# A Strassen stream of split weights: two blocks per x pair, weight sums on the DMA queue, and M2 added onto ScalarE's copy of M1

## The reference

```python
    proj = h @ w_in[l]
...
    x = x + mixed @ w_o[l]
    hx = rmsnorm(x, norm_x_g[l])
    hm = rmsnorm(mem, norm_mem_g[l])
    xq = (hx @ w_xq[l]).reshape(b, s, XATTN_HEADS, XATTN_HEAD_DIM)
...
    x = x + (jax.nn.silu(hf @ w_gate[l]) * (hf @ w_up[l])) @ w_down[l]
```

## Time and profile before

| | us |
|---|---|
| median of 3 runs | 2067.45 (2067.3 to 2068.65) |
| span of the profiled execution, first to last instruction | 2065.9 |
| TensorE matmuls busy | 2054.4, 99% of the span, 9334 instructions |
| VectorE busy | 1667.2 (81%) |
| ScalarE busy | 1181.2 (57%) |
| POOL busy | 50.0 (2%) |

### The profile page before, as it was taken

The page is one execution under the profiler, slowest core; times in us unless marked ns, Lnnn a source line. Parts: engine busy times, 40 slices in busy tenths (PEclk is TensorE's granted clock), DMA queues, the critical chain, the costliest instruction groups (busy, mean ns, idle before and its releaser), DMA issues.

```text
span 2065.9 us, 25348 instructions
## 1 busy us (share of the span) xinstructions
PE 2054.4 (99%) x9334; PEld 1699.8 (82%) x9334; DVE 1667.2 (81%) x1830; ACT 1181.2 (57%) x1533; POOL 50.0 (2%) x84
## 2 busy tenths in 40 slices
PE   9999999999999999999999999999999999999998
PEld 8888888888888888888888888888788888888787
DVE  6877778867766788989889898898777778988875
ACT  7666557656655565555555555555756655654453
POOL 1000000000000000000000000000000000000000
PEclk9999999999999999999999999999999999999999
DMA  9555557655544458777777777776465567789763
GB/s 347 180 172 184 184 180 259 225 182 184 189 158 153 159 185 300 267 259 242 243 237 259 261 242 243 236 270 213 158 214 178 180 201 234 269 285 329 219 197 109
DMA packets 219259, 453.74 MB, mean 220 GB/s; under 512 B 14449, under 2 KB 17153, under 8 KB 219009
## 3 DMA queue, kind: packets, MB, share of 16 engines
q1 hardware_dynamic: 213232, 432.07, 62.9%
q0 software_dynamic: 5616, 19.94, 3.0%
q10 hardware_dynamic: 288, 0.13, 0.0%
HBM read 447.88 MB, written 4.19 MB: 219 GB/s over the span
## 4 chain that ended last, share of the span: by engine, by line
PE 95%; DVE 2%; ACT 1%; issue 1%; DMA 1%; POOL 0%; SPq 0%; DVEq 0%; POOLq 0%; ACTq 0%
PE ps L1117 30%; PE ps L1119 30%; PE ps L1118 29%; PE ps L687 2%; DVE wlo L2494 1%; PE ps L837 1%; PE ps L817 1%; PE ps L921 0%; DMA FR<-in_post_norm_g_dram 0%; PE ps L952 0%; PE ps L963 0%; PE ps L901 0%; DMA FR<-in_x_t_dram 0%; ACT whi L1718 0%; DVE raw L2507 0%
## 5 line engine op out<-in xcount | busy, mean ns | idle before, releaser
L2494 DVE TENSOR_TENSOR wlo<-raw,whi 128x1024 fp32r<-128x1024 f32 x835 | 1010.4, 1222 | 262.8 <-ACT whi L1718 257.4
L1718 ACT ACTIVATE whi<-raw 128x1024 fp32r<-128x1024 f32 x835 | 876.6, 1058 | 564.5 <-PE ps L1119 518.2
L1117 PE MATMUL ps<-whi,bh 128*128 128x512 f32 x1384 | 547.3, 395 | 2.3 <-DVE wlo L2494 2.1
L1119 PE MATMUL ps<-whi,bl 128*128 128x512 f32 x1384 | 539.9, 390 | 0.0
L1118 PE MATMUL ps<-wlo,bh 128*128 128x512 f32 x1384 | 539.2, 390 | 0.0
L1117 PE MATMUL ps<-whi,ah 128*128 128x512 f32 x1080 | 429.3, 398 | 0.2 <-DVE wlo L2494 0.2
L1119 PE MATMUL ps<-whi,al 128*128 128x512 f32 x1080 | 421.6, 390 | 0.0
L1118 PE MATMUL ps<-wlo,ah 128*128 128x512 f32 x1080 | 420.9, 390 | 0.0
L1117 PEld LDWEIGHTS ps<-whi,bh 128*128 128x128 f32 x1384 | 260.1, 188 | 57.0 <-DVE wlo L2494 3.1
L1119 PEld LDWEIGHTS ps<-whi,bl 128*128 128x128 f32 x1384 | 259.8, 188 | 54.7
L1118 PEld LDWEIGHTS ps<-wlo,bh 128*128 128x128 f32 x1384 | 260.2, 188 | 52.5 <-issue 0.2
(11 more groups left out here) (264 smaller groups left out, 1334.6 us busy)
## 6 DMA issues: line engine op xcount, KB each, us to landing
raw<-in_w_in_dram SPq DMA_DIRECT2D x168, 512.0 KB, 4.5
raw<-in_w_ada_dram SPq DMA_DIRECT2D x96, 512.0 KB, 4.6
raw<-in_w_gate_dram SPq DMA_DIRECT2D x88, 512.0 KB, 4.9
raw<-in_w_up_dram SPq DMA_DIRECT2D x88, 512.0 KB, 5.4
raw<-in_w_down_dram SPq DMA_DIRECT2D x88, 512.0 KB, 5.4
raw<-in_w_merge_dram SPq DMA_DIRECT2D x64, 512.0 KB, 5.0
raw<-in_w_o_dram SPq DMA_DIRECT2D x32, 512.0 KB, 4.8
raw<-in_w_xk_dram SPq DMA_DIRECT2D x32, 512.0 KB, 4.7
```

The lines of the kernel that those rows point to most:

```text
L1117: e.matmul(o, xh[:, k, tokens], wh, start=first, stop=False, skip_group_check=more)
L1119: ins = e.matmul(o, xl[:, k, tokens], wh, start=False, skip_group_check=more, stop=kk == 1 and (st.end or st.form in READ))
L1718: done(e.activation(split_at(n)[0], place(item), ACT.Copy), "hi")
L2494: done(e.tensor_tensor(lo, place(stream.entries[n].item), hi.bitcast(F32), ALU.subtract), "lo")
```

## The change

Five things change together.

1. For the pairs of x (kinds tq, v and rg: five pairs) `_pair` lays out **two** Strassen blocks, over chunks 0 and 1, with two of each product, and two chunks instead of three as normal entries. A second set of forms, `x1`, is made for chunk 1 of x. TensorE has 30 matmuls fewer (8610 rows in its program before, 8580 now).
2. Weight sums of the kinds in `QUEUED` are DMAs with an add, issued by POOL (`add_weights`): M5's and M4's, and M6's too in the x pairs. Of 180 sums (160 before) 60 go this way; 120 stay on VectorE. The adding DMA reads both items and writes one of them.
3. In the x pairs four spare item buffers lie in X, which is loaded twice: for its squares, and again after the last spare item is taken.
4. ScalarE copies M1 straight into the bank of the second panel's tile 0, and M2 adds onto it (`start` is left out). The second panel has no `side` any more; it is read straight from PSUM.
5. In pairs of three or two chunks a normal entry stands ahead of M6 and M2.

```diff
+QUADS = {"tq": 2, "v": 2, "rg": 2}
+QUEUED = ("tq", "v", "rg", "o", "xk", "xv", "xq", "xo", "q", "ga", "pu", "gp", "out")
+SPARES = 4
+LANDING = 3
...
+        quads = min(QUADS.get(self.panels[f].kind, 1), chunks - 1)
+        places = [[self._item(p, c, hf) for p, hf in ((f, 1), (f, 0), (s, 0), (s, 1))] for c in range(quads)]
+        todo = iter([(c, hf) for c in range(quads, chunks) for hf in range(2)])
+        at = [{} for _ in range(quads)]
...
+        def product(form, k, start=False, **more):
+            b22, b12, b11, b21 = places[k]
+            item, add = {"M5": (b12, b11), "M3": (b22, None), "M1": (b11, None), "M6": (b22, b12), "M2": (b21, None),
+                         "M7": (b11, b22), "M4": (b21, b22)}[form]
+            at[k][form] = n = self._entry(item, add)
             panel, tile, _, half, _ = PRODUCTS[form]
-            self._step(n, (f, s)[panel], 0, half, (tile,), form, **more)
...
+        if quads == 1:
+            product("M5", 0, start=True, job=False)
+            product("M3", 0, start=True, job=False)
+            normal(f, *next(todo), snap=("s5", q))
+            product("M1", 0, start=True, job=False)
+            if chunks == 4:
+                normal(f, *next(todo), snap=("s1", q))
...
+            product("M5", 0, start=True, job=False)
+            product("M5", 1, job=False)
+            product("M3", 0, start=True)
+            normal(f, *next(todo), snap=("s5", q))
+            product("M3", 1, job=False)
+            product("M1", 0, start=True, job=False)
+            product("M1", 1)
             normal(f, *next(todo), snap=("s1", q))
-            product("M6", b22, b12)
-            product("M2", b21, start=True, snap=("v", q))
-            normal(f, *next(todo))
-            normal(f, *next(todo))
-        else:
-            product("M2", b21, start=True, snap=("s1", q))
-            product("M6", b22, b12)
+            product("M2", 0, job=False)
+            product("M6", 0)
...
+            product("M2", 1, job=False)
+            product("M7", 0)
+            product("M7", 1)
+            normal(f, *next(todo), snap=("s3", q))
+            product("M4", 0, aside=q)
...
+            if quads == 2 and i == 0:
+                product("M4", 1)
...
+        queued = self.panels[f].kind in QUEUED
+        early = 2
+        if self.panels[f - 1].stagger == "first":
+            early = 3 if queued else 1
+        elif queued:
+            early = 1 if q == 0 else 6
+        for k, made in enumerate(at):
+            for form, n in (("M5", made["M5"] - early), ("M6", made["M3"] + 1),
+                            ("M7", made["M1"] + 2 if quads == 1 else made["M6"] + 1),
+                            ("M4", max(made["M2"], made["M6"]) + 1)):
+                self.sums[made[form]] = Sum(n, made, k, form, queued and form in (("M5", "M4") if quads == 1 else ("M5", "M6", "M4")))
...
+        for m, one in self.sums.items():
+            for item in (self.entries[m].item, self.entries[m].add):
+                used(item, (one.before, 1))
+                used(item, (one.before + (LANDING if one.queue else 0), 1))
...
-            at = min(range(RAWS), key=lambda r: (-1, 0) if holds[r] is None else last[holds[r]])
+            fit = [r for r in range(number) if r < RAWS or (self.spares[r - RAWS].first <= first[item][0]
+                                                            and last[item][0] < self.spares[r - RAWS].last)]
+            at = min(fit, key=lambda r: (-1, r < RAWS) if holds[r] is None else last[holds[r]])
...
+        def ready_to_sum(e, m):
+
+            made, form = stream.sums[m].pair, stream.sums[m].form
+            if form == "M5":
+                for item in stream.entries[m]:
+                    e.wait_ge(*loaded(item))
+            else:
+                e.wait_ge(*sum_done(made["M5" if form == "M6" else "M6"]))
+                e.wait_ge(s["lo"], made[{"M6": "M3", "M7": "M1", "M4": "M2"}[form]] + 1)
...
-            which = 2 * role[p][0] + t
-            return None if which == 3 else side[:, which, :]
...
-                if st.form in ("M6", "M4"):
-                    e.wait_ge(s["snap"], 3 * q + (2 if st.form == "M6" else 3))
+                if st.form in ("M2", "M6", "M4"):
+                    e.wait_ge(s["snap"], 3 * q + (3 if st.form == "M4" else 2))
...
-                form, place = {"s5": ("M5", (0, 0)), "s1": ("M1", (1, 0)), "s3": ("M7", (0, 1))}[what]
-                pair, at = stream.pairs[q]
+                form = {"s5": "M5", "s1": "M1", "s3": "M7"}[what]
+                (f, second), at = stream.pairs[q]
                 panel, t = PRODUCTS[form][:2]
                 e.wait_ge(s["half"], at[form] + 1)
-                if q:
-                    e.wait_ge(*side_taken(stream.pairs[q - 1][0][place[0]], place[1]))
-                done(e.activation(side_of(pair[place[0]], place[1]), bank_of(pair[panel], t)[:, :], ACT.Copy), "snap")
+                if what == "s1":
+                    dst = bank_of(second, 0)[:, :]
+                    if stream.nth[second] > 1:
+                        e.wait_ge(*ev_before(second, 0))
+                else:
+                    tile = 1 if what == "s3" else 0
+                    dst = side_of(f, tile)
+                    if q:
+                        e.wait_ge(*side_taken(stream.pairs[q - 1][0][0], tile))
+                done(e.activation(dst, bank_of((f, second)[panel], t)[:, :], ACT.Copy), "snap")
 
...
+                for k in range(4):
+                    ins = e.activation(AF["x1"][:, k, :], XT[1][:, k, :], ACT.Copy, scale=gcols("mix", 1)[k])
                 done(ins, "af")
...
-                summed(p, 0, HH[:, 0, :])
-                e.wait_ge(*ev(p, 0))
-                done(e.scalar_tensor_tensor(HH[:, 0, :], HH[:, 0, :], root_col["r3"][:, 0:1], ZG[:, 0, :], ALU.mult,
-                                            ALU.mult), "hh")
+                took(e.scalar_tensor_tensor(HH[:, 0, :], bank_of(p, 0)[:, :], root_col["r3"][:, 0:1], ZG[:, 0, :],
+                                            ALU.mult, ALU.mult), p, 0)
...
+                add_weights(made_by_mean[of] - 1)
...
+            queued = [m for m in stream.sum_order if stream.sums[m].queue]
+
+            def add_weights(n):
+
+                while queued and stream.sums[queued[0]].before <= n:
+                    m = queued.pop(0)
+                    item, add = stream.entries[m]
+                    ready_to_sum(e, m)
+                    e.dma_start(place(item), place(add), accum_op=ALU.add).then_inc(sum_done(m)[0], 16)
+
+            def load_x():
+
+                for j in range(4):
+                    e.dma_start(X[:, :, j * PW:(j + 1) * PW], x_v[:, :, j * PW:(j + 1) * PW]).then_inc(s[f"x{j}"], 16)
+
...
+            add_weights(stream.end[index["rg", 1]] - 1)
+            for item in stream.last_in_spare.values():
+                wait_taken(e, item)
+            load_x()
...
-                    wait_taken(stream.before[i])
+                    wait_taken(e, stream.before[i])
+                elif stream.place[i] >= RAWS:
+                    e.wait_ge(s["x_sq"], 8)
```

More of the change, by code:

```diff
@@ L77 @@
 Panel = namedtuple("Panel", "kind i w col rows stagger")
-Entry = namedtuple("Entry", "item add minus nth")
-Step = namedtuple("Step", "n p c hf tiles form start end made job taken snap aside")
+Entry = namedtuple("Entry", "item add")
+Step = namedtuple("Step", "n p c hf tiles form quad start end made job taken snap aside")
+Sum = namedtuple("Sum", "before pair quad form queue")
+Spare = namedtuple("Spare", "first last")
 PRODUCTS = {"M3": (0, 0, True, 1, 0), "M5": (0, 1, True, 1, 1), "M1": (1, 1, False, 0, 0),
@@ L438, in form_of @@
 def form_of(key):
[L440 removed]
+    return key[0] if key[0] != "h" and not key[1] else f"{key[0]}{key[1]}"
 def build_program(nc, a, out):
```

255 lines of the change are left out of this document (151 added, 104 removed).

## The result

The changed kernel takes 2084.6 us (median of 4 runs, 2083.2 to 2086.0), the kernel before 2067.95 on the same chip: a ratio of 1.0078, with a 95% interval of 1.0066 to 1.0091. It is slower by 16.6 us; the forecast was 2066.4 and its range ended at 2077.0.

The account below looks back on a forecast made before the run. The kernel was taken as a queue of matmuls bound by TensorE; -6.80 - 0.74 + 1.35 + 4.1 + 1.0 = -1.1 us, so 2066.4 us against a median of 2067.45, with an 8-in-10 range of 2061.0 to 2077.0.

Parts of the forecast that it names:

- -6.80 for 30 matmuls: Five x pairs lose 6 matmuls each, at 0.2267 us per matmul: -6.80 us.
- -0.74 for the gap at 347 us: TensorE's wait for a split behind a weight sum goes, as M4's sum moves to the queue: -0.74 us.
- +1.35 at the start: Four more ScalarE scalings of x ahead of entry 6's split make TensorE wait: +1.35 us, ends 1.2 and 1.7.
- The copy, nothing: ScalarE's copy of M1 replaces one of the same size, covered by a normal entry of 2.72 us: no cost.
- The first M5 sums: First x pair, entries 18 and 19: TensorE stalls for late queued sums, +4.1 us, ends 0 and 9.3.
- B: Time when entry 17's queued M5 sum is there: 54.0 us, from issue at 48.0 and a landing of 6.0.
- The later sums: Later queued sums in four blocks, mostly hidden with 9.8 us left for the tightest landing: +1.0 us, ends 0 and 7.
- an engine that TensorE hardly waits for: VectorE, freed of 40 weight sums (49 us) and the second panel's side adds: worth nothing, with one exception of 0.74 us.
- only two sums come in 42 us: nothing: Pairs with only M5 and M4 queued have larger slack, so their sums were taken to cost nothing.
- late in every block: Rival, chance 0.20: adding DMAs fill the queues, sums land in 11.5 us and stall every x block; 2077.7 us.
- Hidden: Rival, chance 0.24: first stall at entries 16 to 18 under 1 us, nothing stalls later; 2061.8 us.
- the copy waits for its bank: Rival, chance 0.05: ScalarE stands before a bank still being read, 0.3 us a pair, 12 us more; 2078 us.

Follow-up runs that it names:

- m5_before_bias: The changed kernel with the first pair's two M5 sums issued ahead of the c_bias load in GpSimd's queue; 2083.8 us, ratio 1.0074.
- x_sums_dve: The changed kernel with the weight sums of the five x pairs back on VectorE, two blocks kept; 2085.0 us, ratio 1.0081.

## Why the prediction was wrong

- **-6.80 for 30 matmuls, -0.74 for the gap at 347 us:** right. Both are in the trace, and the gap came back where the queue was taken away.
- **+1.35 at the start:** right; the gap after 24.34 us is 1.38.
- **The copy, nothing:** right.
- **"The first M5 sums", +4.1:** the chain of causes was right up to the issue: loads into spare buffers at 41.9 (taken 41.4), items there at 47.1 (47.4), sum issued at 47.7 (48.0). The failed term is the landing, 6.0 taken and 11.9 and 11.1 measured, so B was 58.8 and not 54.0. Entry 16, for which the prediction had no wait, was late as well, by 3.6 us, for the first sum's landing. By the formula given the stall is 58.8 - 50.2 = 8.6; gaps of 3.6, 0.5 and 2.6 us were measured, and 1.2 us for six matmuls at half pace, which had no term. The price in runs is 8.7 to 9.6 us. I chose the calm rows (6.4) for a moment at which SP's stop had dammed up nine loads; the 12.6 us of the earlier trace rows, for loads of this very stretch, was the nearer row, and I had set it aside since SP's standing "has let the engines run dry". That premise held only for the first two of SP's loads, which landed in 3.8 and 4.8 us.
- **"The later sums", +1.0, ends 0 and 7:** measured 5.9 us more of idle time from 100 to 320 us, 7.6 of excess. That the idle time lies in my bounds is luck, as its cause is one that I had priced at nothing. The landing slack of 9.8 us held: sums of 2 columns changed nothing. The step that failed is "an engine that TensorE hardly waits for the earlier trace rows: nothing". I counted VectorE's total (49 us less) and not what it has to do in the 4.1 us of three products in a row (M2, M7, M7): three splits of 1.22, two M7 sums of 1.22 and the difference of 0.68, 6.8 us. Moving the difference and leaving out the M7 sums each took some 2.3 us of the waits away; the 1.07 us for ScalarE before the transpose had no term either.
- **The stage of mem, no term:** +4.0 by excess (0.7 to 4.7 from 400 to 450 us). I wrote "only two sums come in 42 us: nothing", and didn't ask which of GpSimd's loads stand behind a waiting sum. I had named what is queued ahead of M5's sums, and not what is queued behind M4's.
- **The rivals:** *late in every block* (2077.7) came nearest with its time, and its first half (9.6 us for the first wait) is what happened; its second half, M6's sum late in each block, did not happen, and that its 6.8 us are near the 7.6 of the later gaps is chance. *Hidden* and *the copy waits for its bank* fell.

The rule on reducing transfers in the Trainium skill ("Collectives: The Full Stack", section "The bandwidth ceiling: the fold count and why AG ≠ RS ≠ AR") is borne out as engine time. The same queue in the kernel before:
```profile
q0 software_dynamic: 5616, 19.94, 3.0%
```
By the queues' rows q0 grew from 3.0 to 11.8% of the span and by 33.6 MB, 2.1 of them the second load of x: 184 us less some 6 for x, over 60 sums, is 3.0 us of all 16 engines for each 512 KB; a load takes 1278 us / 432 MB, 1.55 us. An adding DMA occupies the engines twice as long as a load. In TensorE's waits it showed only where the engines were full.

## To carry over

A DMA in place of an engine's operation buys throughput and sells latency: it is good where its operands lie ready many microseconds ahead (here 9.8 us held the second M6 sums, which landed in 5.7 to 8.1), and bad behind a wait that has just released a crowd of loads, so put the first such operations of a stage back on the engine. Before you shorten a matmul step, add up the other engines' work in the few steps around it, not over the span: six-matmul steps of 1.36 us leave VectorE 0.14 us beside a split of 1.22. And for each new wait on an in-order queue, list what stands behind it, loads above all; moving the loads ahead only moved the collision.

## What the runs showed of the hardware

- An adding DMA between two SBUF tiles of 512 KB takes 3.0 us of the 16 engines against 1.55 us for a load (both worked out from the queues' rows), and lands in 4.5 to 14.3 us (median 6.7). Cut to 1 KB it still took 8.9 and 6.5 us while nine loads of 512 KB kept the engines full, and 2.0 us at best.
- A GpSimd subtraction of 128x1024 float32 takes 2.58 to 2.86 us in the mean of its groups (VectorE 1.22), and a VectorE operation on SBUF tiles beside it stood still (3.08 us for 0.42). The Trainium skill, "SBUF — State Buffer", section "SBUF: two separate sides", has an exclusive lock on a port pair of the two engines, held for a whole instruction; the trace agrees in that one of the two stood until the other (2.69 us) was done.
- After TensorE had idled 3.6 us, six matmuls ran at half pace (0.43 us apart); in the kernel with single blocks it was eight after each of two waits of 1.8 us, so these cost 1.6 us each beyond their length. The granted clock doesn't fall after each wait of this size: it stayed at 1.00 from 50 to 70 us of m5_before_bias, where TensorE was idle for 6.1 of 20 us, and at 1.00 behind the longest wait of x_sums_dve (2.8 us, until 186 us).
